# The up projection of a decoder layer as a 2x2 block product in seven products instead of eight

## The reference

```
x = x + rmsnorm(mix, norm_mix_post[l])
h = rmsnorm(x, norm_ffn_pre[l])
up = causal_depthwise_conv(h @ w_up[l], conv_w[l], conv_b[l])   # y[t] = sum_k w[k] h[t-2+k] + b, k = 0..2
gate, val = up[..., :D_FF], up[..., D_FF:]
f = (jax.nn.silu(gate) * val) @ w_down[l]
x = x + rmsnorm(f, norm_ffn_post[l])
```

## Time and profile before

| | |
|---|---|
| Median of 3 runs | 2713.7 us |
| Span of the profiled execution | 2714.4 us |
| TensorE busy | 2547.3 us, 94% of the span |
| VectorE, ScalarE, GpSimd busy | 49%, 40%, 17% |
| Mix, TensorE's first to last matmul of line 1132 | 987.4 to about 1192 us |
| Up, first matmul to the end of the last | 1217.8 to 2186.0 us |
| Down, first matmul | 2193.2 us |

### The profile page before, as it was taken

One profiled execution on the slowest core, in us unless ns is written; L12 is line 12 of the kernel. 1 busy time (PEld: TensorE's weight loads), 2 busy tenths in 40 slices (PEclk: granted clock), 3 DMA queues, 4 the chain that ended last, 5 costly groups with the idle time before them and its releaser, 6 DMA issues. The chain is left out here.

```text
span 2714.4 us, 37402 instructions
## 1 busy us (share of the span) xinstructions
PE 2547.3 (94%) x12453; PEld 2097.6 (77%) x12453; DVE 1338.2 (49%) x1748; ACT 1073.7 (40%) x1828; POOL 452.0 (17%) x416
## 2 busy tenths in 40 slices
PE   6989996999999979969999999999999989999997
PEld 5767885778888868757888888888888878787786
DVE  4434223999899957753333333433333333434432
ACT  4311113888888845532222222322222223333322
POOL 0000002776666623310000000000000000101101
PEclk9999997999999989989999999999999999999998
DMA  7922336163333047787111111111111144545453
GB/s 235 287 63 81 127 118 163 33 172 85 80 79 80 17 121 207 218 252 243 39 54 39 58 47 46 54 41 56 39 54 39 51 143 149 189 143 193 142 191 112
DMA packets 248429, 307.97 MB, mean 113 GB/s; under 512 B 11588, under 2 KB 176124, under 8 KB 243708
## 3 DMA queue, kind: packets, MB, share of 16 engines
q1 hardware_dynamic: 243708, 289.81, 34.9%
q0 software_dynamic: 4608, 16.78, 1.5%
HBM read 195.39 MB, written 94.37 MB: 107 GB/s over the span
## 5 line engine op out<-in xcount | busy, mean ns | idle before, releaser
L733 POOL TENSOR_TENSOR weight<-beta,stick 128x512 f32<-128x512 f32 (+3 forms) x320 | 304.9, 960 | 602.5 <-ACT beta L687 448.7
L1295 DVE SCALAR_TENSOR_TENSOR conv<-value_ps,taps,conv 128x512 f32<-128x512 f32 (+2 forms) x176 | 131.3, 746 | 370.0 <-ACT conv L1255 370.0
L1398 POOL TENSOR_TENSOR y<-y,x 128x1024 f32<-128x1024 f32 x16 | 38.9, 2432 | 1448.9 <-DVE y L1457 1448.6
L779 DVE TENSOR_TENSOR_SCAN stick<-z_ps,stick,beta 128x512 f32<-128x512 f32 x192 | 245.5, 1279 | 25.3 <-ACT z_ps L688 24.4
L506 PE MATMUL out_ps<-hT,w_hi 128*128 128x512 f32 x768 | 239.8, 394 | 10.0 <-DVE w_lo L440 10.0
L1255 ACT ACTIVATE conv<-value_ps,taps 128x512 f32<-128x512 f32 x88 | 68.7, 781 | 390.1 <-PE value_ps L1321 390.1
L1321 PE MATMUL gate_ps<-wide,wu_hi 128*128 128x512 f32 x704 | 218.1, 391 | 3.7 <-DMA wide<-h2T_scratch 3.7
L1321 PE MATMUL value_ps<-wide,wu_hi 128*128 128x512 f32 x704 | 216.7, 389 | 0.0
L1295 DVE SCALAR_TENSOR_TENSOR conv<-gate_ps,taps,conv 128x512 f32<-128x512 f32 (+2 forms) x176 | 131.2, 746 | 171.9 <-ACT conv L1255 171.9
L687 ACT ACTIVATE beta<-z_ps 128x512 f32<-128x512 f32 (+3 forms) x320 | 170.9, 534 | 93.4 <-PE z_ps L813 78.7
L830 PE MATMUL wT_ps<-ident,weight 128*128 128x128 f32 x1088 | 174.0, 275 | 12.3 <-POOL weight L733 12.3
(11 more groups left out here) (168 smaller groups left out, 5402.4 us busy)
## 6 DMA issues: line engine op xcount, KB each, us to landing
wu_f<-in_w_up SPq DMA_DIRECT2D x44, 512.0 KB, 5.5
f_scratch<-f SPq DMA_DIRECT2D x88, 256.0 KB, 2.4
bridge<-in_w_down SPq DMA_DIRECT2D x44, 512.0 KB, 3.4
bridge<-f_scratch SPq DMA_DIRECT2D x88, 256.0 KB, 3.7
wd_f<-in_w_down SPq DMA_DIRECT2D x44, 512.0 KB, 3.5
xt<-in_x SPq DMA_DIRECT2D x16, 512.0 KB, 5.7
hT<-h_hi SPq DMA_DIRECT2D x16, 512.0 KB, 4.6
hT<-h_lo SPq DMA_DIRECT2D x16, 512.0 KB, 5.4
```

What stands on the lines that cost most here:

```text
L733: pool.tensor_tensor(weight[v % weight_ring][:, 0:w], beta[v % stick_in][:, 0:w], stick[q % 2][:, at:at + w], ALU.mult).then_inc(weight_do ...
L779: dve.tensor_tensor_scan(stick[q % 2][:, at:at + w][:, ::-1], backwards, beta[u % stick_in][:, 0:w], start, ALU.mult, ALU.bypass).then_inc ...
L1295: dve.scalar_tensor_tensor(out=out, in0=ps[h][:, g * BANK - back + skip:(g + 1) * BANK - back], scalar=column(kind, h, slot), in1=out, op0 ...
L1398: pool.tensor_tensor(y[t][:, :], y[t][:, :], x2[t][:, :], ALU.add).then_inc(added, 1)
```

## The change

**Seven products.** The product of the weights' 2x2 blocks (rows: gate and value; columns: lower and upper half of k) with the hidden state's 2x2 blocks (rows: halves of k; columns: even and odd tiles of 128 tokens) is made with seven block products and sums of operands and results. The up stage has two spans (`part`) of 1024 tokens. A unit u is one block j in one span: 44 units of 7 products, each 4 k x 3 = 12 matmuls of 128x512, in the order of `UP_ORDER`. In all 44 x 84 = 3696. Some products are added up in the PSUM bank of an earlier one (`adds=True`), after another engine has read what was there.

**Left sums.** Of each unit's weights POOL makes four sums s1 to s4 of 128x512. ACT and DVE split seven operands of 128x512 for a unit. As the spans are two, each block's weights are loaded, summed and split twice.

**Right sums.** In mix, ACT copies the turned tile once (`copied`), DVE's `h_lo` is gone, and POOL makes four sums of 128x512 for each pair of tiles. Seven operands are stored in `x7` in place of `h2T`. They are split in up, for each span, 128x2048 at a time (`right_half` on ACT, `right_low` on DVE). At the end of mix POOL also makes the four left sums of unit 0, and ACT and DVE split one right operand and two left ones there (before: the whole first block of weights).

**Results.** DVE adds PSUM results and kept ones (`up_q`, `up_v`) into a tile `up_cols`, in on-chip memory, from which ACT scales 1024 tokens and DVE adds the shifted taps. SP clears 21 semaphores of finished stages in attention, after its first loads.

The core of the diff (in `phase_mix` up to the line with `copied`, then `phase_up`: SP, POOL, ACT, DVE, TensorE):

```diff
...
+                def x_sums(pair):
+                    def total(k, out, plus, other, op):
+                        pool.wait_ge(sums_out, stored(pair, 64))
+                        pool.tensor_tensor(x8[:, out, :, :], x8[:, plus, :, :], x8[:, other, :, :], op).then_inc(x_sum_done, 1)
+                    total(0, t1, b12, b11, ALU.subtract)
+                    total(1, t3, b22, b12, ALU.subtract)
+                    pool.wait_ge(x_sum_done, 4 * pair + 6)
+                    total(2, t2, b22, t1, ALU.subtract)
+                    pool.wait_ge(x_sum_done, 4 * pair + 7)
+                    total(3, t4, b21, t2, ALU.subtract)
...
+                    if is_tile(t - 2) and slot == 1:
+                        pool.wait_ge(copied, done(t - 2))
+                        x_sums(uses - 1)
...
+                        act.activation(x8[:, 2 * slot:2 * slot + 2, :, :].rearrange("p b c t -> p (b c t)"), turn_ps[:, :], ACT.Copy).then_inc(copied, 1)
...
-                    if is_tile(t - 2):
-                        dve.wait_ge(hi_done, done(t - 2))
-                        dve.wait_ge(hT_out[slot], stored(uses - 1, 32))
-                        dve.tensor_tensor(h_lo[slot][:, :, :].rearrange("p c t -> p (c t)"), turn_ps[:, :],
-                                          as_f32(h_hi[slot][:, :, :].rearrange("p c t -> p (c t)")), ALU.subtract).then_inc(lo_done, 1)
...
+UP_ORDER = ("s1t1", "a12b21", "s2t2", "s4b22", "s3t3", "next a11b11", "a22t4")
+UP_LEFT = ("a11", "s1", "a12", "s2", "s4", "s3", "a22")
...
+                    if at_part_end(u, part):
+                        for operand, product in enumerate(("a11b11", "s1t1", "a12b21", "s2t2", "s4b22", "s3t3", "a22t4")):
+                            sp.wait_ge(product_done, multiplied(u, product))
+                            load_x(part + 1, operand)
...
+                    pool.wait_ge(w_in_[e], 32 * pair + 32)
+                    pool.wait_ge(wu_done, split_of(u - 1, "s1"))
+                    pool.tensor_tensor(s1, a21, a22, ALU.add).then_inc(wu_sum_done, 1)
+                    pool.wait_ge(wu_done, split_of(u - 1, "s2"))
+                    pool.wait_ge(wu_sum_done, 4 * u + 1)
+                    pool.tensor_tensor(s2, s1, a11, ALU.subtract).then_inc(wu_sum_done, 1)
+                    pool.wait_ge(wu_done, split_of(u - 1, "s4"))
+                    pool.wait_ge(wu_sum_done, 4 * u + 2)
+                    pool.tensor_tensor(s4, a12, s2, ALU.subtract).then_inc(wu_sum_done, 1)
+                    pool.wait_ge(wu_done, split_of(u - 1, "s3"))
+                    pool.tensor_tensor(s3, a11, a21, ALU.subtract).then_inc(wu_sum_done, 1)
...
+                    left_half(u, e, "a22", pair)
+                    if not first:
+                        value_tap(u - 1, 1 - e)
+                    if start:
+                        right_half(part, 2 if first else 5)
+                    if not last:
+                        left_half(u + 1, 1 - e, "a11", pair + e)
+                    if start:
+                        right_half(part, 3 if first else 6)
+                    if not last:
+                        left_half(u + 1, 1 - e, "s1", pair + e)
+                    act.wait_ge(product_done, multiplied(u, "a12b21"))
+                    if not first:
+                        act.wait_ge(gate_conv, 2 * u)
+                    act.activation(tiles_of(0, 0), tiled(gate_even[e]), ACT.Copy).then_inc(gate_even_done, 1)
+                    if first:
+                        right_half(part, 4)
+                    if not last:
+                        left_half(u + 1, 1 - e, "a12", pair + e)
+                    if ends:
+                        right_half(part + 1, 0)
+                    if first:
+                        right_half(part, 5)
+                    if not last:
+                        left_half(u + 1, 1 - e, "s2", pair + e)
+                    if ends:
+                        right_half(part + 1, 1)
+                    if first:
+                        right_half(part, 6)
+                    if not last:
+                        left_half(u + 1, 1 - e, "s4", pair + e)
+                    act.wait_ge(gate_even_done, u + 1)
+                    act.wait_ge(gate_odd_done, u + 1)
+                    act.wait_ge(taps_done, u + 1)
+                    if not first:
+                        act.wait_ge(f_done, u)
+                    tap(0, e, gate_tap_done)
+                    if ends:
+                        right_half(part + 1, 2)
+                    if not last:
+                        left_half(u + 1, 1 - e, "s3", pair + e)
+                    if ends:
+                        right_half(part + 1, 3)
+                    if not last:
+                        keep_q(u + 1, 1 - e)
+                    act.wait_ge(gate_conv, 2 * u + 2)
+                    act.activation(conv[0][:, :], conv[0][:, :], ACT.Silu).then_inc(silu_done, 1)
+                    if ends:
+                        right_half(part + 1, 4)
...
+                def shifted(h, e, tap_done, u, conv_done):
+                    for back, kind in ((1, 2), (2, 1)):
+                        if back == 1:
+                            dve.wait_ge(tap_done, u + 1)
+                        else:
+                            dve.wait_ge(conv_done, 2 * u + 1)
+                        dve.scalar_tensor_tensor(out=conv[h][:, :], in0=cols[:, h, 2 - back:2 - back + span], scalar=column(kind, h, e),
+                                                 in1=conv[h][:, :], op0=ALU.mult, op1=ALU.add).then_inc(conv_done, 1)
+                def value_even(u, e):
+                    dve.wait_ge(product_done, multiplied(u, "a22t4"))
+                    dve.tensor_tensor(tiles_of(1, 0), tiled(value_chain[e]), tiled(q[e]), ALU.add).then_inc(value_even_done, 1)
...
+                    if not first:
+                        value_even(u - 1, 1 - e)
...
+                    if first:
+                        right_low(part, 2)
+                    left_low(u, e, "a22")
+                    if not first:
+                        shifted(1, 1 - e, value_tap_done, u - 1, value_conv)
+                    if start and not first:
+                        right_low(part, 5)
...
+                    keep_v(u, e)
+                    if not first:
+                        f_of(u - 1, 1 - e, pair - (1 - e))
+                    if not last:
+                        copy_taps((j + 1) if not ends else 0, 1 - e)
+                        left_low(u + 1, 1 - e, "a11")
+                    if start and not first:
+                        right_low(part, 6)
+                    if first:
+                        right_low(part, 4)
+                    if not last:
+                        left_low(u + 1, 1 - e, "s1")
+                    dve.wait_ge(product_done, multiplied(u, "s2t2"))
+                    dve.wait_ge(v_done, u + 1)
+                    dve.tensor_tensor(tiles_of(0, 1), tiled(value_chain[e]), tiled(v), ALU.add).then_inc(gate_part_done, 1)
+                    if first:
+                        right_low(part, 5)
+                    if not last:
+                        left_low(u + 1, 1 - e, "a12")
+                    if ends:
+                        right_low(part + 1, 0)
+                    if not last:
+                        left_low(u + 1, 1 - e, "s2")
+                    if ends:
+                        right_low(part + 1, 1)
+                    dve.wait_ge(product_done, multiplied(u, "s4b22"))
+                    dve.wait_ge(gate_part_done, u + 1)
+                    dve.tensor_tensor(tiles_of(0, 1), tiled(gate_odd_ps[e]), tiles_of(0, 1), ALU.add).then_inc(gate_odd_done, 1)
+                    if first:
+                        right_low(part, 6)
+                    if not last:
+                        left_low(u + 1, 1 - e, "s4")
+                    dve.wait_ge(product_done, multiplied(u, "s3t3"))
+                    dve.tensor_tensor(tiles_of(1, 1), tiled(value_chain[e]), tiled(v), ALU.add).then_inc(value_odd_done, 1)
+                    dve.wait_ge(carried, u + 2 if part > 0 else 1)
+                    dve.wait_ge(gate_odd_done, u + 1)
+                    shifted(0, e, gate_tap_done, u, gate_conv)
+                    if ends:
+                        right_low(part + 1, 2)
+                    if not last:
+                        left_low(u + 1, 1 - e, "s3")
+                    if ends:
+                        right_low(part + 1, 3)
+                        right_low(part + 1, 4)
...
+                def product(bank, left, right, adds=False):
+                    for k in range(half):
+                        for t, (w, x) in enumerate(((a_hi, x_hi), (a_hi, x_lo), (a_lo, x_hi))):
+                            m = pe.matmul(bank[:, :], w[left][:, k, :], x[right][:, k, :],
+                                          start=(not adds and k == 0 and t == 0), stop=(k == half - 1 and t == 2), skip_group_check=adds)
+                    m.then_inc(product_done, 1)
...
```

(32 more changed lines are left out.)

442 lines of the change are left out of this document (282 added, 160 removed).

## The result

| | before | after |
|---|---|---|
| Median of 4 runs each, us | 2712.4 (2710.8 to 2719.2) | 2623.4 (2622.4 to 2624.7) |
| Ratio, 95% interval | | 0.9665 (0.9651 to 0.9679) |
| Span of the profiled execution, us | 2714.4 | 2621.0 |

The change takes 89.0 us off by the medians and 93.4 by the profiled executions; the forecast was 97.7. The two differ because of the executions that were profiled. The median before is 2712.4 here and not 2713.7, because a fourth run has been added.)

What follows compares the result with a forecast made beforehand. TensorE was taken to bound the up stage, a POOL, ACT and DVE ring mix. Up 837.5 + 15 + 15 = 867.5 against 968.2 (-100.7), end +3, mix -5, entry +5: -97.7, so 2616 us; 8-in-10 range 2593 to 2655.

Steps and rivals of the forecast that it cites:

- Matmuls and their pace: Up stage: 528 of 4224 matmuls go; the rest keep 0.2266 us each, 837.5 us if TensorE never waits.
- DVE keeps up: Up stage: DVE's work is 14.9 us in each unit of 19.03, with 1.9 us to spare at `gate_part` and `value_odd`.
- POOL beside DVE: Up stage: POOL's sums hold DVE's two-operand on-chip instructions; 0.7 us a unit on DVE, nothing on TensorE.
- the rival: Up stage: POOL's sums, 5.1 us a unit, delay DVE, which sets the pace at 21.8 us; 2738 us, chance 0.04.
- First unit: Start of up: loads and splits of right operands cost 11 us, slow clock some 4; 15 us, bounds 8 and 25.
- Change of spans: Up, after unit 21: seven right operands loaded and split anew cost 14 us, 15 with a slow start; bounds 4 and 25.
- The clock: Up stage: slow clock in stalls, some 4 us at the first unit; a slow start took unit 22's stall from 14 to 15.
- End of up: Gap from up's last matmul to down's first: 10.3 us where it was 7.2; +3 us, bounds +1 and +5.
- Mix: Mix stage: `h_lo` leaves the ring, POOL's sums delay odd additions by 0 to 4 us; -5 us, bounds -9.6 and +6.
- the forecast's own sign of being wrong: Mix stage: the forecast would be wrong if the odd tiles came later than 13.2 us.
- Entry: From mix to up: POOL's eight sums and waiting for DVE's splits precede the first matmul; +5 us, bounds -1 and +9.
- the drain: Entry to up: the drain of mix's ring of POOL, ACT and DVE was to save about 3 us at the last copy.

Runs made afterwards that it cites:

- experiment 6: Changed kernel with one more DVE addition of 128x1024 in each unit, behind the split of s3: 2626.1 us, ratio 0.9668 to the kernel before.
- experiment 3: Changed kernel with three more DVE additions of 128x1024 in each unit, behind the split of s3: 2727.4 us, ratio 1.0043 to the kernel before.
- experiment 5: Changed kernel with three late DVE additions a unit and POOL's four left sums over one column in 128: 2631.1 us, ratio 0.9691.
- experiment 7: Changed kernel with the product of a12 and b21 over one of its four blocks of k, 75 matmuls a unit: 2545.8 us, ratio 0.9373.
- Experiment 1: Changed kernel with the right operands neither loaded nor split again for the second span: 2606.0 us, ratio 0.9596 to the kernel before.
- experiment 9: Changed kernel with three second-span loads ahead of the next weights' loads and one low half behind `gate_part`: 2617.2 us, ratio 0.9636.
- Experiment 8: Kernel before with only the mix stage's reorder, `h_lo` behind `hn` and mix: 2704.9 us, ratio 0.9959.
- experiment 2: Changed kernel with three more DVE additions of 128x1024 in each unit, in front of `gate_part`: 2779.8 us, ratio 1.0232 to the kernel before.
- experiment 4: Changed kernel with POOL's four left sums of each unit made twice: 2690.0 us, ratio 0.9904 to the kernel before.

## Why the prediction was right

Forecast 2616, measured 2623.4. Sound are the main term, the matmuls at their old pace, and the places where time is lost. The smaller terms are right in part by luck, as said below.

- **Matmuls and their pace**: forecast 837.5 us, from the rows 44 x 19.04 = 837.8. Right.
- **DVE keeps up**: forecast 14.9 us in 19.03; measured 223.13 us busy in 300, 14.2 a unit. `gate_part` is made 8.9 us after the unit's start (9.0 forecast), and from 1471.03 on the waits stand where the order of times put them. Right, and experiment 6 shows that there is room. ACT and POOL are hidden.
- **POOL beside DVE**: forecast 0.7 us for the split of a12, measured 0.1 (0.78 for 0.68). Right in the place, and right that three of the four sums do no harm. The reason that I gave against the rival was wrong, though: "when DVE runs late its waits for TensorE vanish" was meant to bring DVE relief. Experiments 3, 5 and 7 show the opposite: while DVE waits, POOL's sums run beside it for nothing, and once the waits are gone the sums hold DVE's instructions, by 1.9 us a unit in experiment 7 and 3.1 in experiment 3. The rival's mechanism exists, and its 5.1 us a unit was a fair upper bound. What kept it away is slack, at least 1.2 us a unit by experiment 6 and less than the 3.7 us that experiment 3 adds.
- **First unit**: forecast +15, measured 17: waits 9.7 (11 forecast), clock 7.0 (4 forecast).
- **Change of spans**: forecast +15, measured 19.4: waits 14.2 (14 forecast), clock 5.2 (1 forecast). Experiment 1 confirms the whole, 18.7. The waits' sum is right in part by luck: the forecast had x0 fit in, but 3.75 us went to its load, a wait that was gone when experiment 9 issued that load earlier. The clock is the mis-sized term of the sum at both places, 7 us together, and it is most of the 7.9 us by which up's -92.8 falls short of -100.7.
- **End of up**: forecast +3, measured +2.5.
- **Mix**: forecast -5, with up to 4 us of delay by POOL's sums in each odd tile; measured -6.9. Experiment 8 has the same 197 us without the sums, so they take nothing back. The odd addition does come late, and at 13.55 us it passes the forecast's own sign of being wrong (later than 13.2). The sign was badly chosen: the even tile makes up for it (11.14), and TensorE hardly waits.
- **Entry**: forecast +5, measured +6.4. The forecast's own terms don't give 5: 10.2 us of sums and 2 to 3 of waiting in place of 8.7, less 3 for the drain, are about +1. So this figure is near by luck. In the traces the last copy comes 0.8 us earlier, counted from mix's last part product (16.8 against 17.6), and not 3; without POOL's sums it would be 4.5 (13.1, experiment 8). From that copy to the first up matmul 15.9 us pass, against 8.75 before. POOL's eight sums fill 12.9 of them.
- The stages before the change's reach differ by 2.4 us between the two profiled executions. That is chance: in the twelve profiled kernels that have the change and are alike up to there, the first part product of mix starts between 985.04 (after) and 989.61 us, and before it starts at 987.40.

## What to carry to other kernels

When a change gives two engines work that can hold each other up, write the timetable of a unit with the places where the busier one waits for a third. In this kernel those waits, just ahead of PSUM reads, are what hides the other's instructions, and when the slack is used up both the work and the hold are paid. Test the margin in both sizes, one small addition and a large one, since the answer isn't proportional (0 us for one, 103 for three). Price a stall at its length plus the slow stretch behind it.

## What the runs showed of the hardware

- **The clock behind a stall.** In after, after each wait of 2.66 us or more in the up stage (15.96, 2.66, 5.56, 3.75, 9.65 us) the next matmuls ran at the lower level of 1.2 GHz (PEclk 0.50), about 0.43 us apart: the 12 from 1214.77 to 1219.54 took 4.77 us where 2.72 would do, 2 us lost, and the 12 behind the wait of 2.66 us took 4.4, 1.7 lost. So that stall cost 4.4 us. After waits of 1.16 us or less there was no such loss. Windows behind the waits of 5.56, 1.16 and 9.65 us:

```profile
1236.00:1239.00 3.00, 3.00 (x8) 2.32 (x8) 3.00 (x3) 1.74 (x1) 1.98 (x2) 0.50 0.47 114
1245.00:1247.00 2.00, 2.00 (x10) 1.65 (x9) 2.00 (x3) 0.79 (x1) 1.29 (x1) 1.00 0.00 0
...
1681.00:1685.00 4.00, 4.00 (x10) 3.13 (x11) 3.48 (x4) 1.25 (x1) 2.14 (x3) 0.50 0.00 0
```

They hold 8, 10 and 10 matmuls in 3, 2 and 4 us. Between the two the outcome varied: of 21 waits of 2.15 to 2.17 us in experiment 2, 12 were followed by the lower level (0.50 to 0.62 in the window from 1 to 3 us behind the wait) and 9 by 1.00. Two of them, with the second wait just one unit after the first:

```profile
1433.27:1435.27 2.00, 2.00 (x10) 1.68 (x9) 2.00 (x3) 1.25 (x1) 1.29 (x1) 1.00 0.00 0
1454.73:1456.73 2.00, 2.00 (x6) 1.54 (x5) 2.00 (x3) 1.24 (x1) 1.29 (x1) 0.50 0.00 0
```

- **The hold is mutual and depends on alignment.** POOL's sum of 128x512 took 1.28 us alone and 2.21 beside DVE's three additions (experiment 3). The carried columns' copy of 128x4 on DVE, 0.17 us in after, took 0.67 in experiment 4. POOL's same four sums cost DVE about 0.1 us a unit when DVE waits for TensorE, 1.9 at a unit of 17.0 us, when it hardly waits, and 3.1 with three additions more in a unit of 21.2 us, of which 1.0 on those additions.
